# A fused two-block transformer kernel: the expert passes pick the next pass's tokens behind gate-up, from a table of passes

## The reference

```python
grp = jnp.argmax(g_logits, axis=-1)                 # 4 groups of 8 experts
top_v, top_i = lax.top_k(e_in_grp, TOP_K)           # 2 experts of the token's group
weights = (jax.nn.softmax(top_v, axis=-1) * p_grp).reshape(n_asg)
...
def expert_block(args):                             # 32 experts
    xb, e = args
    gate, up = jnp.split(xb @ w_gate_up[e], 2, axis=-1)
    return (jax.nn.silu(gate) * up) @ w_down[e]
...
y = jnp.zeros((n_tok, D), x.dtype).at[tok_s].add(y_buf[dest] * w_s[:, None])
```

## Time and profile before

| | us |
|---|---|
| three runs | 1657.16, 1657.77, 1658.91 (median 1657.77) |
| the profiled execution's own time | 1659.07 |
| its span, from first to last instruction | 1657.3 |
| mean granted TensorE clock | 0.968 of full |
| busy: PE, PEld, DVE, ACT, POOL | 1534.3, 1279.9, 1004.8, 679.7, 361.4 |

### The profile page before, as it was taken

One profiled execution on the slowest core, in us unless ns is written; L12 is line 12 of the kernel. 1 busy time (PEld: TensorE's weight loads), 2 busy tenths in 40 slices (PEclk: granted clock), 3 DMA queues, 4 the chain that ended last, 5 costly groups with the idle time before them and its releaser, 6 DMA issues.

```text
span 1657.3 us, 30527 instructions
## 1 busy us (share of the span) xinstructions
PE 1534.3 (93%) x12376; PEld 1279.9 (77%) x12377; DVE 1004.8 (61%) x1756; ACT 679.7 (41%) x986; POOL 361.4 (22%) x223
## 2 busy tenths in 40 slices
PE   9999987777777677999999999999999999999998
PEld 8889974444444344888889998888888899988887
DVE  5875732222222212888758678866788658788854
ACT  6464421111111110654635755544455436655542
POOL 1120040000000000144204614430344107324410
PEclk9999988898988988999999999999999999999999
DMA  9555699999999999554545455455554545465450
GB/s 351 200 211 209 236 404 430 427 431 433 431 435 429 434 432 425 210 191 172 192 146 189 160 212 191 175 183 212 190 189 167 176 154 197 152 224 188 171 181 26
DMA packets 38007, 421.10 MB, mean 254 GB/s; under 512 B 4410, under 2 KB 6602, under 8 KB 9618
## 3 DMA queue, kind: packets, MB, share of 16 engines
q1 hardware_dynamic: 37234, 415.49, 64.5%
q0 software_dynamic: 672, 4.15, 0.6%
HBM read 416.45 MB, written 3.18 MB: 253 GB/s over the span
## 4 chain that ended last, share of the span: by engine, by line
PE 84%; DMA 8%; DVE 3%; issue 2%; ACT 1%; ACTq 1%; SPq 0%; DVEq 0%
PE bank L1326 19%; PE bank L1343 10%; PE bank L1328 10%; PE bank L1214 7%; PE bank L826 7%; DMA area<-moe_w_dram 7%; PE bank L828 6%; PE bank L827 6%; PE bank L1345 5%; PE bank L1243 3%; PE bank L1140 2%; DVE sq L2575 1%; DMA ring<-first_w_dram 1%; PE bank L1426 1%; PE bank L1439 1%
## 5 line engine op out<-in xcount | busy, mean ns | idle before, releaser
L1326 PE MATMUL bank<-h_split,w_hi 128*128 128x512 f32 x1408 | 489.7, 392 | 0.6 <-DVE h_split L2161 0.6
L1326 PEld LDWEIGHTS bank<-h_split,w_hi 128*128 128x128 f32 x1408 | 264.3, 188 | 59.6 <-DVE h_split L2161 1.2
L1813 ACT CAST w_hi<-ring 128x2048 fp32r<-128x2048 f32 (+2 forms) x124 | 232.8, 1879 | 141.5 <-PE bank L1345 102.7
L721 POOL TENSOR_TENSOR area<-area,stat 128x256 f32<-128x256 f32 x88 | 215.3, 2446 | 294.0 <-DVE area L2652 294.0
L1328 PE MATMUL bank<-h_split,lo_last 128*128 128x256 f32 x840 | 234.8, 280 | 0.0
L2170 DVE TENSOR_TENSOR lo_last<-ring,w_hi 128x2048 fp32r<-128x2048 f32 (+3 forms) x75 | 174.2, 2325 | 6.9 <-ACT w_hi L1813 6.8
L1328 PE MATMUL bank<-h_split,lo_first 128*128 128x256 f32 x568 | 158.8, 280 | 0.0
L1328 PEld LDWEIGHTS bank<-h_split,lo_last 128*128 128x128 f32 x840 | 157.8, 188 | 0.0
L1214 PE MATMUL bank<-ring,sq 128*32 128x256 f32 x1360 | 108.1, 479 | 34.4 <-DVE sq L2575 31.4
L1214 PEld LDWEIGHTS bank<-ring,sq 128*32 128x32 f32 x1360 | 63.2, 136 | 72.9 <-issue 61.5
L2170 DVE TENSOR_TENSOR lo_first<-ring,w_hi 128x2048 fp32r<-128x2048 f32 (+3 forms) x50 | 116.8, 2336 | 2.7 <-ACT w_hi L1813 2.5
(11 more groups left out here) (488 smaller groups left out, 3471.7 us busy)
## 6 DMA issues: line engine op xcount, KB each, us to landing
ring<-moe_w_dram SPq DMA_DIRECT2D x35, 3072.0 KB, 24.7
ring<-layer_w_dram SPq DMA_DIRECT2D x56, 1536.0 KB, 6.5
area<-moe_w_dram SPq DMA_DIRECT2D x18, 3072.0 KB, 26.4
ring<-layer_w_dram SPq DMA_DIRECT2D x32, 1408.0 KB, 6.2
ring<-layer_w_dram SPq DMA_DIRECT2D x34, 1024.0 KB, 5.1
ring<-first_w_dram SPq DMA_DIRECT2D x21, 1536.0 KB, 6.7
ring<-moe_w_dram SPq DMA_DIRECT2D x15, 1536.0 KB, 13.8
area<-moe_w_dram SPq DMA_DIRECT2D x4, 1536.0 KB, 8.8
```

Of the source, the lines that this page charges most:

```text
L721: pool.tensor_tensor(up, up, stat[:, 3, :], ALU.mult).then_inc(S("up_scaled"), 1)
L1326: pe.matmul(halves(first_bank + side), hi_of(q)[:, cols], h_split[:, :, k, :], start=k == 0, stop=False, skip_group_check=True)
L1813: act.copy(hi_of(q)[:, cols], ring[:, PLACES[q % len(PLACES)], cols]).then_inc(S("hi_a_ready"), 1)
```

## The change

A pass no longer begins with its own picking. `pick_tokens(nth + 1)` and `turn_tokens` for the next pass stand behind gate-up, ahead of this pass's down. `combine` (of the previous pass) stays in the pass, behind gate-up. The tokens of the first pass are picked ahead of the loop. Since DVE now must know, in pass n, the expert and window of passes n + 1 and n + 2, a table `plan` is made ahead of the loop: for each pass its expert, and the number of passes before that expert. PE makes it with three small matmuls (one cumulative sum of `passes_of`, then two with `ended`), DVE with one comparison, ACT copies it. DVE and ACT then run one loop over all passes instead of a loop in a loop, and DVE reads the table four times in each pass (two for `selected`, two for `shared`). Behind the last pass one more pass is picked and moved, and not used. The weights' transfers, the pairs and the slots are as before.

```diff
@@ PE, ahead of the loop
             pe.matmul(ps[0][0:1, 352:352 + EXPERTS], passes_of[:, 0:1], strict[0:EXPERTS, 0:EXPERTS],
-                      start=True, stop=True).then_inc(S("starts_done"), 1)
+                      start=True, stop=True).then_inc(S("planned"), 1)
+            pe.matmul(ps[3][0:EXPERTS, 400:401], const("tri", EXPERTS)[:, 0:EXPERTS], passes_of[:, 0:1],
+                      start=True, stop=True).then_inc(S("planned"), 1)
@@ PE, a pass
-            def expert_pass(nth, e, turn):
-
-                pe.wait_ge(S("share_t_ready"), nth)
+            def pick_tokens(nth):
                 pe.wait_ge(S("select_ready"), nth)
...
-                pe.wait_ge(S("picked_ready"), nth)
-                settled(pe)
+            def turn_tokens():
                 for side in range(2):
                     m = pe.transpose(ps[1][:, P * (1 + side):P * (2 + side)], picked[:, side, :], ident)
                 m.then_inc(S("picked_turned"), 1)
-                if e == 0:
-                    keep_clock(1, 0)
+            def expert_pass(nth, e, turn, passes_end=None):
...
                 m.then_inc(S("up_done"), 1)
...
+                pe.wait_ge(S("share_t_ready"), nth)
+                pick_tokens(nth + 1)
+
+                pe.wait_ge(S("hid_ready"), nth)
+                settled(pe)
+                pe.transpose(ps[1][:, 0:P], two["hid"], ident).then_inc(S("hid_turned"), 1)
                 pe.wait_ge(S("y_ready"), nth)
                 settled(pe)
                 combine(False)
                 pe.wait_ge(S("share_ready"), nth)
+                pe.wait_ge(S("picked_ready"), nth + 1)
                 settled(pe)
                 for j in range(TT):
                     m = pe.transpose(ps[2][:, T + j * P:T + (j + 1) * P], share[:, j, :], ident)
                 m.then_inc(S("share_turned"), 1)
-
-                pe.wait_ge(S("hid_ready"), nth)
-                settled(pe)
-                pe.transpose(ps[1][:, 0:P], two["hid"], ident).then_inc(S("hid_turned"), 1)
                 pe.wait_ge(S("hid_t_ready"), nth)
                 settled(pe)
+                turn_tokens()
@@ PE, ahead of the first pass
+            pick_tokens(1)
+            pe.wait_ge(S("spread_copied"), 1)
+            keep_clock(1, 1)
+            pe.wait_ge(S("planned"), 3)
+            pe.matmul(ps[3][0:1, 408:408 + PASSES + 1], ones[0:EXPERTS - 1, 0:1], ended[0:EXPERTS - 1, :], ...)
+            pe.matmul(ps[3][0:1, 457:457 + PASSES + 1], passes_of[:, 0:1], ended, ...).then_inc(S("planned"), 1)
+            pe.wait_ge(S("picked_ready"), 1)
+            turn_tokens()
+            keep_clock(1, 0)
@@ ACT
+            copy_picked(1)
+            act.wait_ge(S("planned"), 4)
+            act.copy(plan[0:1, :], ps[3][0:1, 408:408 + 2 * (PASSES + 1)]).then_inc(S("planned"), 1)
+            expert_pass(1)
+            packed = act.value_load(meta[0:1, EXPERTS - 1:EXPERTS], ...)
+            with act.Fori(1, total_passes(packed)) as n:
+                expert_pass(n + 1)
@@ DVE
-            with dve.Fori(1, EXPERTS) as e:
-                expert(e)
+            selected(0, 0)
+            dve.wait_ge(S("planned"), 2)
+            ts(ended, const("count", EXPERTS), ps[3][0:EXPERTS, 400:401], None, ALU.is_ge).then_inc(S("planned"), 1)
+            picked_moved(1)
+            def planned(n):
+                e = dve.value_load(plan[0:1, bass.ds(n, 1)], ...)
+                before = dve.value_load(plan[0:1, bass.ds(n + PASSES + 1, 1)], ...)
+                first = nc.s_assert_within((n - before) * P, 0, (WINDOWS - 1) * P, ...)
+                return e, first
+            dve.wait_ge(S("planned"), 5)
+            selected(*planned(1))
+            dve.wait_ge(S("shares_made"), 1)
+            shared(0, 0)
+            hidden(1)
+            picked_moved(2)
...
+            with dve.Fori(1, total_passes(packed)) as n:
+                selected(*planned(n + 1))
+                shared(*planned(n))
+                hidden(n + 1)
+                picked_moved(n + 2)
```

More of the change, by code:

```diff
@@ L69 @@
 WIN = 32
+PASSES = EXPERTS + T * TOP_K // WIN
 PAIRED = 8
@@ L248, in program @@
         meta = sb("meta", [1, 2 * EXPERTS], I32)
+        plan = sb("plan", [1, 2 * (PASSES + 1)], I32)
         lbs = sb("lbs", [P, 24])
@@ L516, in program, with total_passes @@
         last_parts = (spare_landed[2], 1), (spare_landed[3], 1), (layer_full[4], 2)
+        def total_passes(packed):
+            return nc.s_assert_within(packed // 16 + packed % 16, EXPERTS, PASSES,
+                                      skip_runtime_bounds_check_because="T tokens have TOP_K experts each")
         def moe_slot(m):
@@ L1255, in expert @@
                     expert_pass(before + w + 1, e, turn)
+            pick_tokens(1)
+            pe.wait_ge(S("spread_copied"), 1)
+            keep_clock(1, 1)
+            pe.wait_ge(S("planned"), 3)
+            pe.matmul(ps[3][0:1, 408:408 + PASSES + 1], ones[0:EXPERTS - 1, 0:1], ended[0:EXPERTS - 1, :],
+                      start=True, stop=True)
+            pe.matmul(ps[3][0:1, 457:457 + PASSES + 1], passes_of[:, 0:1], ended, start=True, stop=True)\
+                .then_inc(S("planned"), 1)
+            pe.wait_ge(S("picked_ready"), 1)
+            turn_tokens()
+            keep_clock(1, 0)
             passes_end = pe.alloc_register("first_passes")
             with pe.Fori(0, passes_end) as w:
-                expert_pass(w + 1, 0, 0)
+                expert_pass(w + 1, 0, 0, passes_end)
             for e in range(1, LOOP_AT):
@@ L1787, in expert_pass @@
                 act.copy(y, ps[3][:, 0:T].rearrange("p (s n) -> p s n", s=2)).then_inc(S("y_ready"), 1)
[L1789 to L1801 removed]
+            copy_picked(1)
+            act.wait_ge(S("planned"), 4)
+            act.copy(plan[0:1, :], ps[3][0:1, 408:408 + 2 * (PASSES + 1)]).then_inc(S("planned"), 1)
+            expert_pass(1)
+            packed = act.value_load(meta[0:1, EXPERTS - 1:EXPERTS], min_val=1,
+                                    max_val=16 * (EXPERTS + ASSIGNED // WIN) + WINDOWS)
+            with act.Fori(1, total_passes(packed)) as n:
+                expert_pass(n + 1)
             act.copy(lbs[:, 0:1], lbs[:, 4:5]).then_inc(S("moe_done"), 1)
@@ L2545, in _ @@
             for choice, where in enumerate((e1, e2)):
-                own.mark(tt(where, over(const("expert"), TT), over(best_at[:, :, choice], EXPERTS, 2), ALU.is_equal))
+                own.mark(tt(where, over(const("count")[:, 0:EXPERTS], TT), over(best_at[:, :, choice], EXPERTS, 2), ALU.is_equal))
             own.wait()
@@ L2594, in _ @@
             dve.wait_ge(S("iota_loaded"), 16)
-            passes_end = dve.alloc_register("first_passes")
-            with dve.Fori(0, passes_end) as w:
-                first = nc.s_assert_within(w * P, 0, (WINDOWS - 1) * P,
-                                           skip_runtime_bounds_check_because="an expert has at most T tokens")
-                selected(0, first)
-                picked_moved(w + 1)
-                dve.wait_ge(S("shares_made"), 1)
-                shared(0, first)
-                dve.wait_ge(S("meta_ready"), 1)
-                dve.reg_mov(passes_end, dve.value_load(meta[0:1, 0:1], min_val=1, max_val=WINDOWS))
-                hidden(w + 1)
@@ L2607, in expert @@
-            def expert(e):
-                packed = dve.value_load(meta[0:1, bass.ds(e, 1)], min_val=1,
-                                        max_val=16 * (EXPERTS + ASSIGNED // WIN) + WINDOWS)
-                before, passes_r = packed // 16, packed % 16
-                with dve.Fori(0, passes_r) as w:
-                    first = nc.s_assert_within(w * P, 0, (WINDOWS - 1) * P,
-                                               skip_runtime_bounds_check_because="an expert has at most T tokens")
-                    selected(e, first)
-                    shared(e, first)
-                    picked_moved(before + w + 1)
-                    hidden(before + w + 1)
@@ L2620, in _ @@
-            with dve.Fori(1, EXPERTS) as e:
-                expert(e)
+            selected(0, 0)
[3 more added lines that the diff above has]
+            def planned(n):
+                e = dve.value_load(plan[0:1, bass.ds(n, 1)], min_val=0, max_val=EXPERTS - 1)
+                before = dve.value_load(plan[0:1, bass.ds(n + PASSES + 1, 1)], min_val=0, max_val=PASSES)
+                first = nc.s_assert_within((n - before) * P, 0, (WINDOWS - 1) * P,
+                                           skip_runtime_bounds_check_because="an expert has at most T tokens")
+                return e, first
@@ L2895, in constant_tables @@
         "rev_group": np.tile(np.arange(GROUPS, 0, -1), (P, 1)),
-        "expert": np.tile(np.arange(EXPERTS), (P, 1)),
+        "count": np.tile(np.arange(PASSES + 1), (P, 1)),
         "bucket": np.concatenate([by_distance, np.zeros((P - BUCKETS, T))]),
```

29 lines of the change are left out of this document (9 added, 20 removed).

## The result

The changed kernel takes 1666.81 us (median of 5 runs, 1665.27 to 1667.1) against 1657.70 (5 runs, 1657.16 to 1658.91): a ratio of 1.0052 with an interval of 1.0038 to 1.0065. It is slower by about 9 us, and the forecast of 1657.3 (1654.9 to 1660.8) was wrong. The profiled execution took 1666.16 us with a span of 1664.3, 7.0 more than before; the medians are 9.1 apart, as the profiled execution of the kernel before was a slower one (1659.07).

What follows compares the result with a forecast made beforehand. The prediction took the experts' weights' stream, at a DMA share of 1.00, to bound the stage. Its terms summed as 0 + 0 + 0.1 - 0.6 = -0.5 us, from 1657.77 to 1657.3 us, range 1654.9 to 1660.8.

Steps and rivals of the forecast that it cites:

- What follows the last pass: Residual, norm and second block after the experts' stage: they move with the last pass's end, no cost of their own.
- The stream bounds the stage: Experts' stage: the weights' transfers fill the DMA engines (share 1.00, 431 to 432 GB/s) and set its end.
- The shorter pass: Passes not waiting for weights get some 2.5 us shorter (nearer 4 at full clock); value for the end time 0.
- about four experts: Weights loaded ahead in ring and spare slots; PE gains 1.2 us a pass and eats this lead by about 505 us.
- DVE's loads: Four register loads a pass, estimated 2.0 us where 0.5 were, hidden behind gate-up and picking: 0.
- The first pass: Start of the experts' stage: first gate-up 0.1 us later, adding +0.1 us; bounds -0.4 and +2.0.
- The last pass: End of the experts' stage: gate-up follows the slots, down begins earlier; -0.6 us taken, bounds -1.4 and +2.7.
- the stream depends on the passes: Sign of a wrong forecast: the last third's landing moves more than 2 us either way from 658.7 us.
- The low clock: Rival, last pass: starved PE stays at the low clock through down, +4.7 us, 1662.5 us in all; chance 0.09.
- The first pass didn't stall the stream: Rival, first pass: DVE 2 us late with the table, all transfers shift by up to 2.0, 1659.3 us; chance 0.10.
- denser: Rival, weights' stream: earlier refills win the 0.45 us dry spell and 1 us more, 1654.9 us; chance 0.05.
- The pass is the bound: Rival, experts' stage: 20 passes lose 2.5 us or more each, -50 us, 1608 us; chance 0.02.

Runs made afterwards that it cites:

- a1: The changed kernel with all tiles at the addresses of the kernel before (`plan` behind `area`, `consts` at its old width): 1658.62 us against 1657.53.
- h1: The kernel before, with whole-pair refills of the experts' weights loading only the first of two slots (output not the reference's): 1644.38 us, ratio 0.9922.
- h2: The changed kernel on the old addresses, with whole-pair refills loading only the first of two slots (output not the reference's): 1516.27 us, ratio 0.9147.
- l2: The kernel before with 64 unused bytes behind `consts`, so all later tiles move together; its total time isn't in the text, its last third landed at 661.6 us.
- r1: The changed kernel with only `plan` moved behind `area`, `consts` staying wide: 1660.52 us, ratio 1.0011.

## Why the prediction was wrong

The step that failed is "*What follows the last pass* (residual, norm, second block) moves with it", a cost of 0. It does move with it, but it also gets longer by itself, by 6.5 us in the profiled execution. Behind it is a term that the list of parts doesn't have at all: the change adds a tile and widens another, and every tile behind them moves. The diff shows both, `plan` and `count`, and the working counted the instructions that use them and not the bytes that they take. The rest of the kernel is not neutral to that.

*The stream bounds the stage.* Right. The share stayed at 1.00, the waits turned from DVE to weights, a1 made no difference, and h1 and h2 show 128 us hidden under the stream.

*The shorter pass.* Its value for the end, 0, was right, its size was not: 4.8 us (13.33 to 8.52), not 2.5 to 4. Up to 1.7 of them are the clock, as gate-up takes 3.66 us where it took 5.35. PE met the stream at 294 us; 300 to 350 was forecast. The lead of "about four experts", 58 us of stream, doesn't fit the working's own 20 passes at 1.2 us, 24 us; the working took the one for the lead and the other for when it is gone.

*DVE's loads.* Hidden, as forecast: the second gate-up begins at 244.06, with no wait.

*The first pass.* The first gate-up came 0.9 us late and not 0.1. In a1 it is 234.75, 0.1 late, and in the shifted kernels it lies between 233.8 and 236.9 with the old instructions too, so the 0.9 isn't shown to be a cost of the new matmuls.

*The last pass.* On the old addresses (a1) the last down ends at 661.24 us, 1.6 before (660.87 + 1.94), a little past the bound of -1.4. That is mostly luck: in this execution the last third landed at 657.5 us, 1.3 earlier than in the earlier trace rows, and the lag of down behind it only went from 2.1 to 1.9. The last pass was at the low level for its first two parts, 1.94 and 1.96 us instead of 1.07:

```profile
653.82 1.94 PE L1217 MATMUL bank<-ring,sq 128*32 128x256 f32 x16 [1.33 <-DMA ring<-moe_w_dram]
655.50 1.96 PE L1199 MATMUL bank<-vtok,sq 128*32 128x256 f32 x16
...
659.31 1.93 PE L1250 MATMUL bank<-ring,sq 128*32 128x256 f32 x32
```

The medians of the runs (1658.62 against 1657.53) show no gain, so none is claimed. In the changed kernel as it stands the last third landed 2.5 us later, which is the mark that the prediction named for "the stream depends on the passes". The passes aren't the reason: l2 has the old ones and lands its last third at 661.6. The slower pace with the ring 64 B off accounts for some 1.6 us, and the stage began 0.9 later.

*The rivals.* None was it. The low clock didn't come in the changed kernel (1.00 from 640 to 664 us); in a1 it came for part of the last pass. The first pass didn't stall the stream, and the stream got thinner, not denser. "The pass is the bound" was given 0.02, and rightly: the shorter pass is worth 128 us where the refills bring half the bytes, and nothing where they don't (a1). The Trainium skill, "Perfetto Trace Analysis", section "Optimization Strategies", says to optimise the engines that TensorE waits for on the critical path. The trace agrees with it in h1 and h2 (the 128 us), and not where the weights come whole.

*The range.* It held only costs of instructions and transfers. Its upper end, 1660.8, would have held r1 (1660.52) and not the kernel as written.

What stays open: why a matmul slows with the distance of its operands, why only some of them do at most distances, and why the changed instructions lose 2.0 us more than the old ones on the same addresses. That the reads of tokens and weights meet in the same part of SBUF at some distances would fit a pattern that repeats after 256 B, but no run isolates it. Distances of 160 and 192 B against 416 and 448 weren't tried, nor whether the ring's place repeats after 256 or only after 512 B. No version that loads all weights beat the kernel before.

## What to carry to other kernels

Count the bytes of a change as well as its instructions: a tile that is added or widened moves all behind it, and the distance of two large tiles that a matmul reads together can be worth more than the change itself (0.4% here). Where time is lost in code that the diff doesn't touch, compare the mean ns of the same group in both pages before looking for a wait, and put unused tiles into the old kernel to test it. Put small new tiles behind the large ones. Where a stage is bound by a full stream, a shorter chain on the engines is worth nothing until the stream is made lighter.

## What the runs showed of the hardware

- Matmuls of 512 columns took 229.2 ns on average, or 230.0 to 236.6 with another distance in SBUF between their operands (32 to 448 B more), at a granted clock of 1.00; 256 B more cost nothing. The longer ones come in a regular beat (229 and 240 ns in turn with 64 B more). Over the kernel's second block this is 4 to 13 us of 977, in one trace of each kernel.
- The 3072 KB transfers landed every 7.27 to 7.28 us or every 7.31 us by where in SBUF they are written (0 and 512 B, or 64 and 128 B from the old place), at a DMA share of 1.00 in both.
- One register load by DVE from SBUF took 0.30 us, and four of them in a pass stayed hidden.
